# A transformer block's forward pass in split fp32: order of weight conversions, a PSUM bank's return, the start and the last norm

## The reference

```python
rms_norm_2(x, final_norm_2)   # x * rsqrt(mean(x*x) + 1e-6) * gain, per token
```

## Time and profile before

| what | us |
|---|---|
| median of 3 runs | 2548.75 (2548.26 to 2549.3) |
| the profiled execution | 2547.44 |
| its span, first to last instruction | 2545.7 |
| PE busy | 2517.0 |
| DVE busy | 1871.6 |
| ACT busy | 1171.7 |
| POOL busy | 195.2 |

### The profile page before, as it was taken

How to read it: one execution, slowest core, us unless ns; L and a number is a source line. 1 busy time by engine, 2 the same in 40 slices (tenths; PEclk the granted TensorE clock), 3 DMA queues, 4 the chain that set the end, 5 groups by cost and what they waited for, 6 DMA issues and landing times.

```text
span 2545.7 us, 31653 instructions
## 1 busy us (share of the span) xinstructions
PE 2517.0 (99%) x11647; PEld 2099.3 (82%) x11647; DVE 1871.6 (74%) x2329; ACT 1171.7 (46%) x1611; POOL 195.2 (8%) x199
## 2 busy tenths in 40 slices
PE   8999999999999999999999999999999999999998
PEld 7888888878888888888888888888888888878887
DVE  7988358889883599843556999449985479799853
ACT  6445226664453444532225545335553337654531
POOL 0000004500000000000000000000000044100000
PEclk9999999999999999999999999999999999999999
DMA  7765232156753367543333675445764321367542
GB/s 220 165 165 137 89 87 77 34 153 160 178 111 104 122 170 172 126 113 100 100 94 113 177 167 125 116 129 140 167 135 126 93 89 42 108 150 170 135 117 80
DMA packets 508952, 321.81 MB, mean 126 GB/s; under 512 B 287488, under 2 KB 435712, under 8 KB 508800
## 3 DMA queue, kind: packets, MB, share of 16 engines
q1 hardware_dynamic: 499296, 285.19, 40.5%
q0 software_dynamic: 9504, 34.61, 8.0%
HBM read 248.68 MB, written 2.10 MB: 99 GB/s over the span
## 4 chain that ended last, share of the span: by engine, by line
PE 92%; DVE 5%; ACT 1%; issue 1%; DMA 1%; SPq 0%; POOLq 0%; POOL 0%; DVEq 0%; ACTq 0%
PE pair L577 30%; PE pair L579 30%; PE pair L578 30%; DVE wl L1634 1%; PE pair L793 1%; ACT wh L1162 0%; DMA part<-raw 0%; DVE a_mx L1865 0%; DVE Xl L1644 0%; PE pair L868 0%; PE pair L869 0%; DVE X L1644 0%; PE pair L626 0%; DVE a_RB L1644 0%; ACT Xh L1190 0%
## 5 line engine op out<-in xcount | busy, mean ns | idle before, releaser
L1634 DVE TENSOR_TENSOR wl<-raw,wh 128x1024 fp32r<-128x1024 f32 (+2 forms) x547 | 647.0, 1187 | 414.5 <-ACT wh L1162 412.6
L1162 ACT ACTIVATE wh<-raw 128x1024 fp32r<-128x1024 f32 (+2 forms) x547 | 561.7, 1030 | 727.1 <-PE pair L579 689.3
L577 PE MATMUL pair<-Hh,wl 128*128 128x512 f32 (+1 forms) x1061 | 408.5, 385 | 0.0
L579 PE MATMUL pair<-Hh,wh 128*128 128x512 f32 (+1 forms) x1061 | 408.3, 385 | 0.0
L578 PE MATMUL pair<-Hl,wh 128*128 128x512 f32 (+1 forms) x1061 | 408.3, 385 | 0.0
L577 PE MATMUL pair<-wh,Xl 128*128 128x512 f32 (+2 forms) x976 | 375.3, 385 | 11.2 <-ACT Xh L1193 7.6
L577 PE MATMUL pair<-wh,Sl 128*128 128x512 f32 x960 | 373.7, 389 | 0.9 <-DVE wl L1634 0.8
L578 PE MATMUL pair<-wl,Xh 128*128 128x512 f32 (+2 forms) x976 | 373.8, 383 | 0.0
L579 PE MATMUL pair<-wh,Xh 128*128 128x512 f32 (+2 forms) x976 | 373.7, 383 | 0.0
L578 PE MATMUL pair<-wl,Sh 128*128 128x512 f32 x960 | 373.5, 389 | 0.0
L579 PE MATMUL pair<-wh,Sh 128*128 128x512 f32 x960 | 373.5, 389 | 0.0
(11 more groups left out here) (322 smaller groups left out, 3240.2 us busy)
## 6 DMA issues: line engine op xcount, KB each, us to landing
raw<-in_ffn_w_gate SPq DMA_DIRECT2D x120, 512.0 KB, 5.4
raw<-in_ffn_w_up SPq DMA_DIRECT2D x120, 512.0 KB, 4.4
raw<-in_ffn_w_down SPq DMA_DIRECT2D x114, 512.0 KB, 3.8
part<-raw POOLq DMA_DIRECT2D x60, 512.0 KB, 5.8
H<-H SPq DMA_DIRECT2D x288, 64.0 KB, 3.8
H<-squares SPq DMA_DIRECT2D x192, 64.0 KB, 2.2
raw<-in_c_w_in SPq DMA_DIRECT2D x24, 512.0 KB, 3.8
raw<-in_w_in SPq DMA_DIRECT2D x10, 512.0 KB, 3.8
```

What stands on the lines that cost most here:

```text
L577: e.matmul(o, ll, rh, start=start, stop=False, skip_group_check=again)
L579: i = e.matmul(o, lh, rh, start=False, stop=stop, skip_group_check=again)
L1162: e.activation(part_of(n, wh), source_of(n), ACT.Copy).then_inc(whi.up(("w", n)), 1)
L1634: e.tensor_tensor(part_of(n, wl), source_of(n), part_of(n, wh).bitcast(F), ALU.subtract).then_inc(wlo.up(("w", n)), 1)
```

## The change

1. Start: the two DMAs of weight chunk 0 and the one of the gain are issued by ScalarE, ahead of its table load, and no longer by SP. PE begins with 14 products of a 128x128 tile of ones by itself.
2. Attention: `use()` stands at steps listed in `converts`: 2, 8, 14, 20 for mA, where before one stood in the queries, one after them and one each at k = 0, 8, 16; and 1, 6, 12, 18, 24 for mB, where before two stood ahead of the loop and three at k = 4, 12, 20. `mixer_out` calls `use()` earlier by one or two tiles. The totals are the same.
3. In mA (causal) the "out" bank is returned one step later.
4. Last norm: sums of acc are made earlier; part 1's factor product follows five products of ones, and a second such product fills a bank ("row") that ScalarE copies to SBUF. ScalarE multiplies tiles 0 and 1 of part 1 by the gain; GpSimd multiplies them by the factors, and VectorE scales tiles 2 to 7 alone. SP writes part 1's pairs in the order 2, 0, 4, 6.

```diff
-        mA = Mixer(2, True, 8, 2, aP, ...
-        mB = Mixer(8, False, 6, 1, gP, ...
+        mA = Mixer(2, True, 8, 2, (2, 8, 14, 20), aP, ...
+        mB = Mixer(8, False, 6, 1, (1, 6, 12, 18, 24), gP, ...
...
+                def early_sums(part):
+                    bank = take(LAST[part][1], ("stat", 10, part))
+                    w.wait_ge(dve, ("sq", s))
+                    for i in range(2):
+                        q = slice(HALVES[part][0] + 128 * i, HALVES[part][0] + 128 * i + 128)
+                        e.matmul(bank[:, i:i + 1], acc[s % 2][:, q], ones[:, 0:1], start=i == 0, stop=True, skip_group_check=i > 0)
...
                 def factors(part):
                     name = ("rb", 10, part)
                     bank = take(LAST[part][2], name)
+                    for _ in range(5 * part):
+                        e.matmul(bank[:, 0:128], ones[:, :], ones[:, :], start=True, stop=True)
                     w.wait_ge(dve, ("diag", 10, part))
                     e.matmul(bank[:, 0:256], ones[:, :], fdiag[part][:, :], start=True, stop=True).then_inc(mm.up(name), 1)
+                    if part == 1:
+                        w.wait_ge(dve, ("var", 10, 0))
+                        e.matmul(banks[LAST[0][1]][:, 0:256], ones[:, :], fdiag[1][:, :], start=True, stop=True).then_inc(
+                            mm.up(("row", 10)), 1)
...
-                    if m.put_at(k) is not None:
-                        free(("out", s, m.put_at(k)))
+                    h = m.put_at(k - 1 if m.causal else k)
+                    if h is not None:
+                        free(("out", s, h))
...
+            w.wait_ge(pool, "ones")
+            for _ in range(14):
+                e.matmul(banks[4][:, 0:128], ones[:, :], ones[:, :], start=True, stop=True)
...
# ScalarE and VectorE, attention
-                    t = m.early_at(k, 0)
-                    if t is not None and t % 2 == 0:
+                    if k in m.converts:
                         use()
...
# ScalarE, mixer_out
-                    if t == 2:
+                    if t % 2 == 0:
                         use()
...
-                    if t == 6:
-                        use()
...
# VectorE, mixer_out
-                    if t in (2, 4):
+                    add_to_x(s, t, banks[bank_of["down", s, t]], ("down", s, t), ("x", s, t))
+                    if t in (1, 3, 5):
                         use()
-                    add_to_x(s, t, banks[bank_of["down", s, t]], ("down", s, t), ("x", s, t))
...
-                use()
...
# ScalarE, start and last norm
+            for dst, src in moves_of(0):
+                e.dma_start(dst, src).then_inc(raw_in[loads[0].slot].sem, 16)
+            e.dma_start(gain0[:, :], a["par"][:, 0:KT]).then_inc(gain_in.sem, 16)
...
+                if part == 0:
+                    for t in range(2):
+                        copy(fin[:, t, 256:512], X[:, t, 256:512], ("scaled", t), scale=col("final", t))
+            w.wait_ge(mm, ("row", 10))
+            copy(rb[0][:, 0:256], banks[LAST[0][1]][:, 0:256], ("row", 10))
...
# GpSimd
+            w.wait_ge(act, ("row", 10))
+            for t in range(2):
+                w.wait_ge(act, ("scaled", t))
+                tt(fin[:, t, 256:512], fin[:, t, 256:512], rb[0][:, 0:256], ALU.mult, ("fin", t, 1))
...
# SP
-            e.dma_start(gain0[:, :], a["par"][:, 0:KT]).then_inc(gain_in.sem, 16)
...
-                for t in range(0, KT, 2):
-                    w.wait_ge(dve, ("fin", t + 1, part))
+                for t in ((0, 2, 4, 6), (2, 0, 4, 6))[part]:
+                    w.wait_ge(pool if t == 0 and part == 1 else dve, ("fin", t + 1, part))
```

More of the change, by code:

```diff
@@ L376, in Hh, with moves_of @@
             return Hh0[:, k, :] if k < 16 else Hh16[:, k - 16, :] if k < 20 else Hh20[:, k - 20, :]
+        def moves_of(n):
+            moves, width, nk, r, _ = loads[n]
+            for row, (c0, c1), k0, src in moves:
+                dst = raw[r][row:row + src.shape[0], 0:nk * width].rearrange("p (k n) -> p k n", n=width)
+                yield dst[:, k0:k0 + src.shape[1], c0:c1], src
         def source_of(n):
@@ L446, in build, with __init__ @@
         class Mixer:
-            def __init__(self, s, causal, ahead, early, P, tiles, stats):
-                self.s, self.causal, self.ahead, self.early = s, causal, ahead, early
+            def __init__(self, s, causal, ahead, early, converts, P, tiles, stats):
+                self.s, self.causal, self.ahead, self.early, self.converts = s, causal, ahead, early, converts
                 self.P, (self.PTh, self.PTl) = P, tiles
@@ L473, in q_rows @@
                 return slice(64 * (h % 2), 64 * (h % 2) + 64)
-        mA = Mixer(2, True, 8, 2, aP, (aRB[:, 0:4, :], aRB[:, 4:8, :]), (amx, anb, aL, aLi))
-        mB = Mixer(8, False, 6, 1, gP, (gRB[:, 0:4, :], gRB[:, 4:8, :]), (gmx, gnb, gL, gLi))
+        mA = Mixer(2, True, 8, 2, (2, 8, 14, 20), aP, (aRB[:, 0:4, :], aRB[:, 4:8, :]), (amx, anb, aL, aLi))
+        mB = Mixer(8, False, 6, 1, (1, 6, 12, 18, 24), gP, (gRB[:, 0:4, :], gRB[:, 4:8, :]), (gmx, gnb, gL, gLi))
         def qk(m, h):
@@ L649, in last_tile @@
                 rows = []
+                def early_sums(part):
[4 more added lines that the diff above has]
+                        e.matmul(bank[:, i:i + 1], acc[s % 2][:, q], ones[:, 0:1], start=i == 0, stop=True, skip_group_check=i > 0)
                 def sums(part):
                     name = ("stat", 10, part)
-                    bank = take(LAST[part][1], name)
-                    w.wait_ge(dve, ("sq", s))
+                    bank = banks[LAST[part][1]]
                     w.wait_ge(act, ("fsq", part))
@@ L657, in sums @@
                         q = slice(HALVES[part][0] + 128 * i, HALVES[part][0] + 128 * i + 128)
-                        e.matmul(bank[:, i:i + 1], acc[s % 2][:, q], ones[:, 0:1], start=True, stop=False)
-                        e.matmul(bank[:, i:i + 1], fsq[:, q], ones[:, 0:1], start=False, stop=True).then_inc(mm.up(name), 1)
+                        e.matmul(bank[:, i:i + 1], fsq[:, q], ones[:, 0:1], start=False, stop=True,
+                                 skip_group_check=True).then_inc(mm.up(name), 1)
                 def factors(part):
@@ L679, in last_tile @@
                                 *([name] if k == 21 else []))
+                        if part == 1 and k == 5:
+                            early_sums(0)
                         if part == 1 and k == 6:
@@ L683, in last_tile @@
                             factors(0)
+                        if part == 1 and k == 18:
+                            early_sums(1)
                 sums(1)
@@ L1440, in queries @@
                 def queries(g):
-                    use()
+                    if g < 2:
+                        use()
                     h0, nh = QGROUPS[g]
@@ L1567, in later @@
                     mixed(3)
-                    for _ in range(5):
+                    for _ in range(7):
                         yield
[L1570 to L1573, removed]
                 attention(mB, prepare, later())
                 mixer_out(s, "ffn2_2")
+            for dst, src in moves_of(0):
+                e.dma_start(dst, src).then_inc(raw_in[loads[0].slot].sem, 16)
+            e.dma_start(gain0[:, :], a["par"][:, 0:KT]).then_inc(gain_in.sem, 16)
             w.wait_ge(pool, "ones")
@@ L2390, in vector_program @@
             last_norm(1)
-            last_scale(1, range(KT))
+            last_scale(1, range(2, KT))
         def gpsimd_program(e, w):
@@ L2571, in fetch @@
             def fetch(n):
-                moves, width, nk, r, before = loads[n]
+                r, before = loads[n].slot, loads[n].before
                 if isinstance(before, int):
@@ L2578, in fetch @@
                         w.wait_ge(event, before)
-                for row, (c0, c1), k0, src in moves:
-                    dst = raw[r][row:row + src.shape[0], 0:nk * width].rearrange("p (k n) -> p k n", n=width)
-                    e.dma_start(dst[:, k0:k0 + src.shape[1], c0:c1], src).then_inc(raw_in[r].sem, 16)
+                for dst, src in moves_of(n):
+                    if n > 0:
+                        e.dma_start(dst, src).then_inc(raw_in[r].sem, 16)
                     raw_in[r].n += 16
```

## The result

The changed kernel takes 2552.11 us (median of 20 runs, 2549.87 to 2556.26) against 2548.68 us (20 runs, 2547.26 to 2550.01): a ratio of 1.0014, 95% interval 1.0008 to 1.0020. It is slower by 3.4 us, where 2.5 us less was forecast, and above the stated range. 3.4 us is within the 0.2% that the prediction calls the same, but its sign is clear. The runs also spread wider than those of before, 6.4 us against 2.8. The profiled execution took 2554.2 us, 2.1 above its median, with a span of 2552.4 us.

A forecast was written before the change was run, and what follows sets the result against it. PE, 99% busy, was taken as the bound, leaving stalls at six places. Terms -0.7 + 3.5 - 2.0 - 1.0 - 1.5 - 0.8 = -2.5 us on 2548.75 gave 2546.2 us, range 2538.5 to 2551.5.

The forecast's parts named there:

- mA, forecast +3.5: Attention of stage 2: later bank return lengthens four cycles by 1.03 us to 10.05, conversions moved; sum +3.5 us.
- 0.5 us credited for later waits: In mA: an estimated 0.5 us gain, as lost time covers later short waits.
- Everything else I cost at nothing, because PE is busy above it: All places outside the six with stalls, feed-forward stages included: no change in time, as PE has work there.
- Start, forecast -0.7: Kernel start: earlier loads save 0.7 us; ends 0 and 3.2 gain.
- PE's first product at 6.6 us: Kernel start: PE's first real product moves from 7.56 to about 6.6 us.
- Way into stage 3, forecast -2.0: mixer_out of mA: earlier conversions cover three PE waits, -2.0 us; ends 0 and -2.3.
- Stage 9, forecast -1.5: mixer_out of mB: waits of 0.73 and 1.64 us go, sum of squares limits, -1.5 us; ends 0 and -2.6.
- mB, forecast -1.0: Attention of stage 8: 2.0 us of waits go, conversions at k=6 and k=18 cost 0.5 each; -1.0 us.
- Last norm, forecast -0.8: End of kernel: earlier factor product and shared scaling bring last issue from 2543.41 to 2542.65, -0.8 us.
- The early sums: Last norm: making sums of acc early takes two pairs of products, 0.45 us in all, off PE's chain.
- A: Rival in mA: the later bank return works, no new wait; mA -3.3, total 2539.5 us; chance 0.33.
- B: Rival in mA: turned_low also waits behind conversions, four cycles take 11.2 us, total 2554.5 us; chance 0.10.

The follow-up runs named there:

- experiment 4: Changed kernel plus six 128-column products of ones ahead of the scores of steps 16, 20, 24 and 28 of mA: 2548.70 us, ratio 1.0006.
- experiment 9: Kernel before plus 14 products of ones with one output column each, ahead of all: 2550.79 us, ratio 1.0010.
- experiment 10: Kernel before with weight chunk 0 and the gain issued by ScalarE, without the 14 products: 2547.56 us, ratio 0.9999.
- experiment 6: Kernel before with the start alone (ScalarE issues weight chunk 0 and the gain, 14 products of ones): 2550.63 us, ratio 1.0011.
- experiment 1: Changed kernel with the out bank returned in the step of put again, the rest as changed: 2546.31 us, ratio 0.9991.
- experiment 5: Kernel before with the conversions' new places alone, in both attentions and both mixer_out: 2543.53 us, ratio 0.9982.
- experiment 2: Kernel before with the later return of the out bank alone: 2553.54 us, ratio 1.0020.
- experiment 7: Kernel before with the last norm's change alone: 2548.50 us, ratio 1.0002.

## Why the prediction was wrong

By the single parts, the later bank return costs 5.8 us, the start 2.8, the conversions give 4.3 and the tail is within its interval of nothing: +4.3 in sum, with the +3.4 of the changed kernel near it.

- **mA, forecast +3.5, was +7.4 in the profiled run.** The mechanism stood: first_half waits for turned_low(4m-1), released 1.64 us after put (1.65 said). The term was mis-sized. At full clock the cycles are 10.2 to 10.3 us (10.05 said), and 11.3 with the conversion at k = 14. Left out was that PE can come back from such a wait at the lower level: 2 of 4 times in the profiled run, behind waits of 1.25 and 1.95 us, 1.6 us each, shown by experiment 4. The 0.5 us credited for later waits did not come. The stretches at the lower level account for most of the difference, and they do not fall behind every wait, which fits the wider spread of the runs.
- **"Everything else I cost at nothing, because PE is busy above it" is the step that failed outright.** Stages 3 to 7 gave +2.8 us. Each of the 14 products brings two passes with a weight load each, 56 instructions (PE's count is 11687 against 11647, weight loads apart: 28 here and 12 in the last norm); the fetch near 167 us came near 161 with experiment 9. PE has no idle time near 1742 before, but the chain of transfer, ScalarE and VectorE that feeds it has little slack there, so 1.1 to 1.5 us more on that one transfer are 1.1 to 1.5 us on PE. Elsewhere it has slack: in the kernel before itself a transfer issued at 1846 us takes 7.2 us with a fetch on it, 6.2 without one in other traces, and PE does not stand. The Trainium skill, Runtime: NRT & Kernel Launch, section Instruction fetch mechanics, says that instructions come in blocks of 16 KB, 256 of them, and are fetched ahead; by that 56 of 256 of the some 28 us between two fetches is an estimate of 6 us, and the trace's 167.2 to 161.5 agrees. That the added instructions cost the time is shown by experiments 9 and 10; that they do it by a fetch that slows the transfer it falls on rests on which traces have both, and on shifting the fetch (experiments 9 and 4), not on taking it away.
- **Start, forecast -0.7.** By 56 us it was -0.1 in the changed kernel and -1.4 in experiment 6 (-1.3 and -0.8 in experiments 1 and 4, with the same start). The range held these; the step that failed is PE's first product at 6.6 us. X tile 0, issued 0.45 us earlier, landed at 4.2 us, not before the 3.95 of the kernel before; and the gain, whose arrival was not looked at, queued behind the weights and held X's high part until 6.64 us (5.4 to 5.8 in the four other traces with that issue).
- **Way into stage 3, forecast -2.0, was -2.5. Stage 9, forecast -1.5, was -0.8**, and -1.5 in experiment 5; the sum of squares became the wait, as said there.
- **mB, forecast -1.0, was 0**, in the changed kernel and in experiment 5: the waits came back in full.
- **Last norm, forecast -0.8, was 0.** The early sums were counted as 0.45 us saved, but they only move: PE makes them ahead of its last products, which everything waits for (the offset to before grows by 0.45 us near 2534, and shrinks by as much at the sums). And the landing of the last transfer, which the prediction took as unchanged, came 0.4 us later behind its issue: the span ends 2.7 us after it in all eight traces with the new last norm and 2.2 to 2.3 in the six without. There its neighbours are issued closer ahead of it; that this is the cause is not shown.

Of the rivals, A is refuted by experiments 1 and 2. B, the longer cycle, came nearest in number, with cycles of 11.89, 11.32 and 11.90 us, past its 11.05, and with conversions that gave more than half of theirs; but its mechanism, conversions ahead of turned_low in more than one cycle, is not what made them long: that was the conversion at k = 14 in the second and the lower level in the other two.

## What to carry to other kernels

Where buffers are handed out in a queue, write out who gets which after a change in the order of returns: a buffer given back later does not wait less, it hands its wait to another taker, and the new releaser may stand further down its engine's program. Price a wait of the matrix engine with the slower clock behind it, not by its length alone. And an edit of a few instructions on a long unrolled program moves the fetches of all that follow; try each part alone, and look for losses in stages that it does not touch.

## What was not expected of the hardware

- The clock fell behind waits of 1.25 and 1.95 us and not behind those of 1.42 and 1.41 us in the same run; in the trace of experiment 7 it fell behind one of 1.16 us in mB, which the kernel before has at the same length and at full clock. So the length of a wait alone does not tell. Filling PE with products of ones held the clock at 1.00 in mA's loop and took 1.6 us off each of the two cycles.
- One fetch of 16 KB of instructions goes with 0.2 to 1.1 us more on the 512 KB transfer of GpSimd's queue at 159 us that it falls on (6.2 us without, 6.4 to 7.3 with), and with 1.1 to 1.5 us more on the one at 1732 us (5.8 without, 6.9 to 7.3 with).
- A 4 KB load issued behind two 128 KB loads of the same queue was awaited until 6.6 us, 5.0 us after its issue at 1.66 (3.7 to 4.1 us in four other traces); as SP's first it took 1.7 us before.
